# Where the stationary arrays of a two-layer trunk begin in SBUF, taken by 512 bytes

## The chip, the cores and the metric

One Trainium2 chip, of which the kernel uses one core. The metric is the device time of one execution in microseconds (us). All operands are float32 in memory; the large matmuls read them in the rounded form float32r, one pass of the array per matmul.

## The reference

A decoder trunk with 256 tokens and width 2048: one layer of gated linear attention with a SwiGLU, then shared keys and values, one layer of differential attention and a second SwiGLU. Everything is fp32. Nearly all of the arithmetic is the product of the normalised tokens with weight matrices:

```python
def swiglu(h, w_in, w_out):
    g, u = jnp.split(h @ w_in, 2, axis=-1)
    return (jax.nn.silu(g) * u) @ w_out

# layer 0: proj = rms_norm(x) @ w_in   (2048 x 6160), chunked gated attention, @ w_out (2048 x 2048)
# between: kv = rms_norm(x) @ w_kv      (2048 x 4096)
# layer 1: rms_norm(x) @ w_q (2048 x 2048), differential attention, @ w_out (2048 x 2048)
# each layer: x = x + swiglu(rms_norm(x), ffn_w_in, ffn_w_out)   (2048 x 11264, 5632 x 2048)
```

## The kernel before

Weights come from HBM in units of 256 rows by 512 columns (2 tiles of 128 rows, 512 KB) into a ring of four slots, `raw`. To keep fp32 accuracy with float32r, each number is split in two: ScalarE writes the rounded part into `w_hi` (line 945), VectorE the remainder into `w_lo` (line 1311). The activations are split in the same way and stand turned, features on the partitions, in five stationary arrays `[128, 2, tiles, 256]`: the second axis is high part and low part, the last the tokens. They are `xT` (normalised tokens, for all products from the residual stream except the query's), `g_oT` (output of the first attention), `hT` (the hidden layer of both SwiGLUs, 44 tiles), `xT_q` (the tokens for the query) and `d_oT` (output of the second attention). A line of `[128 tokens]` fp32 is 512 bytes in each partition, and a moving tile of `w_hi` or `w_lo` is 2048.

One unit is 2 tiles x 2 halves of the tokens (`tb`) x 3 matmuls: high x high, high x low, low x high. There are 784 units: gla_in 96, gla_out 32, ffn_in0 176, ffn_out0 88, diff_in 96 (of which 32 read `xT_q`), diff_out 32, ffn_in1 176 and ffn_out1 88. `unit` (lines 633 to 642) issues them:

```python
hi = src[:, 0, kt + j, tb * P:(tb + 1) * P]
lo = src[:, 1, kt + j, tb * P:(tb + 1) * P]
nc.tensor.matmul(acc[p][tb][:, :], hi, w_hi[:, slot, j, :], start=(kt + j == 0), stop=False)
nc.tensor.matmul(acc[p][tb][:, :], hi, w_lo[:, slot, j, :], start=False, stop=False)
last = nc.tensor.matmul(acc[p][tb][:, :], lo, w_hi[:, slot, j, :], start=False, ...)
```

The first operand is the stationary one; it is loaded ahead of each matmul by an instruction of its own (LDWEIGHTS, which the profile lists under PEld), and the second moves. In the trace's names `acc<-w_hi,xT` is the moving operand first, then the stationary.

Small matmuls of the attention parts stand between units: `gate_low` (line 727; moving `xT` 256 columns, stationary `a_w` 96 columns of a tile of 384 bytes), `gate_full` (740; moving `a_T`, stationary `w_gate`, 128 columns), `gla_scores` (762, 767, 770), `gla_output` (780 to 782; plain fp32, 512 columns), `scores` (882, 884), `diff_output` (898 to 900). The order on each engine is written out by hand, with semaphores.

Memory is given out in the order of the declarations, each at a multiple of 32 bytes. `place(name, rest)` declares a gap so that the next array begins at the remainder `rest` modulo 512; `ExitStack`s let arrays of later stages take the place of earlier ones. In the program before, `xT` begins at byte 33280, `raw` at 66048, `w_hi` at 82432, `w_lo` at 98816, `hT` at 128512, `g_oT` at 180224, `xT_q` and `d_oT` at 184832 and `a_w` at 161792: all at remainder 0 by 512.

Of the kernel before, what the change touches and what calls it, by code (L numbers as in the profile page):

```python
# [182 lines left out]
def trunk(nc, x_in, attn_norm, gla_w_in, w_alpha2, b_alpha, gla_head_norm, gla_w_out, kv_norm, w_kv, k_norm,  # L183
          diff_norm, diff_w_q, q_norm, lq1, lk1, lq2, lk2, diff_head_norm, diff_w_out, ffn_norm, ffn_w_in,
          ffn_w_out, const_in, out):
    with ExitStack() as ctx:
        def sb(name, shape, dt=F32, stack=ctx):
            return stack.enter_context(nc.sbuf_tensor(name, shape, dt))
# [4 lines left out]
        def place(name, rest, stack=ctx):  # L193

            base = -(-nc.sbuf_base // 32) * 32
            gap = (rest - base) % 512
            if gap:
                sb(name, [P, gap // 4], F32, stack)


        place("gap_x", 0)
        x = sb("x", [P, TB, D])
        xT = sb("xT", [P, 2, KT, S], F32R)
        raw = sb("raw", [P, SLOTS, UNIT_KT, CB])
        w_hi = sb("w_hi", [P, SLOTS, UNIT_KT, CB], F32R)
        w_lo = sb("w_lo", [P, SLOTS, UNIT_KT, CB], F32R)
# [27 lines left out]
        with ExitStack() as s1:  # L234
            tables = sb("tables", [P, C_COLS - C_MASK], F32, s1)
            g_at = sb("g_at", [P, H_G, 3, P], F32, s1)
            g_r = sb("g_r", [P, TB, DV], F32, s1)
            g_v = sb("g_v", [P, 2, TB, HV], F32, s1)
            a_raw = sb("a_raw", [P, KT, RANK], F32, s1)
            a_w = sb("a_w", [P, KT, GATE_ROWS], F32R, s1)  # L240
            a_T = sb("a_T", [GATE_ROWS, S], F32R, s1)
            a_full = sb("a_full", [GATE_ROWS, S], F32, s1)
            gate_raw = sb("gate_raw", [GATE_ROWS, DK], F32, s1)
            w_gate = sb("w_gate", [GATE_ROWS, DK], F32R, s1)
            lam_rows = sb("lam_rows", [P, 4, HD], F32, s1)
            with ExitStack() as s2:
                g_q = sb("g_q", [P, FT, S], F32, s2)
                g_k = sb("g_k", [P, FT, S], F32, s2)
                log_a = sb("log_a", [P, 2, FT // 2 * S], F32, s2)
                cum = sb("cum", [P, 2, S], F32, s2)  # L250
                ends = sb("ends", [P, 2, 8], F32, s2)
                rstd_diag = sb("rstd_diag", [P, TB, P], F32, s2)
                rstd_row = sb("rstd_row", [GATE_ROWS, S], F32, s2)
                ones = sb("ones", [P, GATE_ROWS], F32, s2)
                k_next = sb("k_next", [P, FT, TB, CHUNK], F32, s2)
                k_far = sb("k_far", [P, FT, P], F32, s2)
                q_far = sb("q_far", [P, FT, P], F32, s2)
            place("gap_g", 0, s1)
            g_oT = sb("g_oT", [P, 2, KT, S], F32R, s1)
        with ExitStack() as s1:  # L260
            place("gap_h", 0, s1)
            hT = sb("hT", [P, 2, FKT, S], F32R, s1)
            x_turned = sb("x_turned", [P, 2, TB, CB], F32, s1)
        with ExitStack() as s1:
            d_q = sb("d_q", [P, 2 * H_D, S], F32, s1)
            d_k = sb("d_k", [P, 2 * H_D, S], F32, s1)
            d_at = sb("d_at", [P, H_D, 3, P], F32, s1)
            d_v = sb("d_v", [P, 2, TB, CB], F32, s1)
            probs = sb("probs", [P, 2, 3 * P], F32, s1)
            place("gap_d", 0, s1)  # L270
            with ExitStack() as s2:
                xT_q = sb("xT_q", [P, 2, KT, S], F32R, s2)
            d_oT = sb("d_oT", [P, 2, KT, S], F32R, s1)
            q_squares = sb("q_squares", [P, TB * CB], F32, s1)
            p_squares = sb("p_squares", [P, 6 * P], F32, s1)
            p_turned = sb("p_turned", [P, 6 * P], F32, s1)
# [1474 lines left out]
```

## Time and profile before

| | |
|---|---|
| time, median of 2 runs | 2196.14 us (2196.1 to 2196.19) |
| span of the profiled execution | 2193.8 us |
| TensorE matmul, busy | 2188.1 us (100%), 9720 instructions |
| TensorE weight load, busy | 1808.9 us (82%), 9720 |
| VectorE / ScalarE / GpSimd, busy | 1242.7 (57%) / 1058.2 (48%) / 283.0 us (13%) |
| read from HBM | 414.37 MB, 190 GB/s over the span |
| granted TensorE clock | full in all 40 slices |

Matmuls overlap: the next one starts before the last one's drawn end, so that a busy share of 100% says only that there are no gaps. What the engine delivers is read from the distance between starts.

### The profile page before, as it was taken

The numbers are of one execution on the slowest core, as the hardware profiler recorded it, in microseconds if no ns is written. First come the engines' busy times: TensorE is split into PE (matmuls) and PEld (weight loads), VectorE is DVE, ScalarE is ACT, GpSimd is POOL, SyncE is SP. The second block draws the span as 40 slices with busy tenths as digits, with TensorE's granted clock in tenths as the row PEclk, the third lists the DMA queues.
The fourth block names the chain that finished last, engine by engine and source line by source line (L and its number), as shares of the span: only waits on it lengthen the run. The fifth ranks groups of instructions, "written<-read, shape, count | busy, mean of one in ns | idle before, by whom it ended". The sixth has DMA issues, their size and how long they took to land.

```text
span 2193.8 us, 27239 instructions
## 1 busy us (share of the span) xinstructions
PE 2188.1 (100%) x9720; PEld 1808.9 (82%) x9720; DVE 1242.7 (57%) x1460; ACT 1058.2 (48%) x1428; POOL 283.0 (13%) x563
## 2 busy tenths in 40 slices
PE   9999999999999999999999999999999999999999
PEld 7888788888888888888888888888888888888887
DVE  5665566655555555555566676665555555555443
ACT  6666455444444444444456665554444444444333
POOL 3210334100000000001125333341000000000000
PEclk9999999999999999999999999999999999999999
DMA  8765667666666666666667666676666666666664
GB/s 264 210 189 176 189 202 218 203 215 203 203 202 213 201 202 206 200 205 203 201 202 217 196 207 202 204 223 210 199 207 200 215 200 203 205 210 194 195 193 163
DMA packets 252675, 447.01 MB, mean 204 GB/s; under 512 B 27665, under 2 KB 41969, under 8 KB 252593
## 3 DMA queue, kind: packets, MB, share of 16 engines
q1 hardware_dynamic: 236176, 428.79, 62.2%
q0 software_dynamic: 16240, 17.07, 2.7%
q8 instruction: 49, 0.80, 0.1%
q14 instruction: 34, 0.27, 0.0%
q10 hardware_dynamic: 176, 0.07, 0.0%
HBM read 414.37 MB, written 2.10 MB: 190 GB/s over the span
## 4 chain that ended last, share of the span: by engine, by line
PE 100%; DVE 0%; ACT 0%; issue 0%; POOL 0%; DVEq 0%; ACTq 0%; POOLq 0%
PE acc L641 32%; PE acc L639 32%; PE acc L640 32%; PE acc L651 1%; PE acc L656 0%; PE side L884 0%; PE tps L678 0%; PE side L727 0%; PE side L703 0%; PE side L762 0%; PE side L882 0%; PE side L898 0%; PE side L899 0%; PE side L900 0%; PE side L782 0%; PE side L780 0%
## 5 line engine op out<-in xcount | busy, mean ns | idle before, releaser
L1311 DVE TENSOR_TENSOR w_lo<-raw,w_hi 128x1024 fp32r<-128x1024 f32 x784 | 954.8, 1222 | 835.6 <-ACT w_hi L945 831.3
L945 ACT ACTIVATE w_hi<-raw 128x1024 fp32r<-128x1024 f32 x784 | 827.8, 1059 | 1002.9 <-PE acc L641 994.0
L639 PE MATMUL acc<-w_hi,xT 128*128 128x512 f32 x2016 | 787.6, 391 | 0.0
L641 PE MATMUL acc<-w_hi,xT 128*128 128x512 f32 x2016 | 784.4, 389 | 0.0
L640 PE MATMUL acc<-w_lo,xT 128*128 128x512 f32 x2016 | 784.4, 389 | 0.0
L639 PEld LDWEIGHTS acc<-w_hi,xT 128*128 128x128 f32 x2016 | 378.4, 188 | 79.0 <-issue 0.7
L640 PEld LDWEIGHTS acc<-w_lo,xT 128*128 128x128 f32 x2016 | 378.4, 188 | 78.9 <-issue 0.7
L641 PEld LDWEIGHTS acc<-w_hi,xT 128*128 128x128 f32 x2016 | 378.4, 188 | 78.9
L639 PE MATMUL acc<-w_hi,hT 128*128 128x512 f32 x700 | 272.3, 389 | 0.0
L640 PE MATMUL acc<-w_lo,hT 128*128 128x512 f32 x700 | 272.3, 389 | 0.0
L641 PE MATMUL acc<-w_hi,hT 128*128 128x512 f32 x700 | 272.3, 389 | 0.0
L640 PEld LDWEIGHTS acc<-w_lo,hT 128*128 128x128 f32 x700 | 131.4, 188 | 27.5
L639 PEld LDWEIGHTS acc<-w_hi,hT 128*128 128x128 f32 x700 | 131.4, 188 | 27.3
L641 PEld LDWEIGHTS acc<-w_hi,hT 128*128 128x128 f32 x700 | 131.4, 188 | 27.1
L588 POOL DMA_DIRECT2D x_turned<-scratch x32 | 15.7, 500 | 580.5 <-DVE scratch L1336 580.5
L588 POOL DMA_DIRECT2D tok<-scratch x112 | 54.9, 499 | 143.2 <-DVE scratch L1336 99.5
L1560 DVE TENSOR_TENSOR hT<-tok,hT 128x512 f32 (+1 forms) x44 | 28.4, 688 | 67.1 <-ACT hT L1140 67.1
L1140 ACT ACTIVATE hT<-tok 128x512 f32 (+1 forms) x44 | 25.4, 624 | 64.1 <-DMA tok<-scratch 64.1
L639 PE MATMUL acc<-w_hi,xT_q 128*128 128x512 f32 x128 | 50.6, 396 | 0.0
L639 PE MATMUL acc<-w_hi,g_oT 128*128 128x512 f32 x128 | 50.2, 392 | 0.0
L639 PE MATMUL acc<-w_hi,d_oT 128*128 128x512 f32 x128 | 50.0, 391 | 0.0
L641 PE MATMUL acc<-w_hi,xT_q 128*128 128x512 f32 x128 | 49.9, 390 | 0.0
(204 smaller groups left out, 1372.2 us busy)
## 6 DMA issues: line engine op xcount, KB each, us to landing
raw<-in_ffn_w_in SPq DMA_DIRECT2D x352, 512.0 KB, 3.8
raw<-in_ffn_w_out SPq DMA_DIRECT2D x176, 512.0 KB, 4.7
raw<-in_gla_w_in SPq DMA_DIRECT2D x96, 512.0 KB, 4.3
raw<-in_w_kv SPq DMA_DIRECT2D x64, 512.0 KB, 4.6
raw<-in_gla_w_out SPq DMA_DIRECT2D x32, 512.0 KB, 4.9
raw<-in_diff_w_q SPq DMA_DIRECT2D x32, 512.0 KB, 4.6
raw<-in_diff_w_out SPq DMA_DIRECT2D x32, 512.0 KB, 4.9
tok<-scratch SPq DMA_DIRECT2D x352, 32.0 KB, 2.9
```

Of the source, the lines that this page charges most:

```text
L588: pool.dma_start(dst[g * SQ:(g + 1) * SQ, s], src[s * SQ:(s + 1) * SQ, g]).then_inc(turn_moved[TURN[name, n] % 2], 16)
L639: nc.tensor.matmul(acc[p][tb][:, :], hi, w_hi[:, slot, j, :], start=(kt + j == 0), stop=False)
L640: nc.tensor.matmul(acc[p][tb][:, :], hi, w_lo[:, slot, j, :], start=False, stop=False)
L641: last = nc.tensor.matmul(acc[p][tb][:, :], lo, w_hi[:, slot, j, :], start=False, stop=(kt + j == n_kt - 1))
L651: nc.tensor.matmul(acc[p][tb][:, :], src[:, part, kt + j, tb * P:(tb + 1) * P], w_hi[:, slot, j, :], start=(kt + j == 0 and part == 0), st ...
L945: nc.scalar.activation(w_hi[:, slot, :, :], raw[:, slot, :, :], ACT.Copy).then_inc(hi_done, 1)
L1140: nc.scalar.activation(hidden(0, n, tb), turned(tb), ACT.Copy).then_inc(h_hi, 1)
L1311: nc.vector.tensor_tensor(w_lo[:, slot, :, :], raw[:, slot, :, :], w_hi[:, slot, :, :].bitcast(F32), ALU.subtract).then_inc(lo_done, 1)
L1560: nc.vector.tensor_tensor(hidden(1, n, tb), turned(tb), hidden(0, n, tb).bitcast(F32), ALU.subtract).then_inc(h_lo, 1)
```

## The change

Three more gaps are declared, and two that were there get another remainder. In the program after, `xT` begins at byte 33344 (64 by 512), `raw` at 66560, `w_hi` at 82944, `w_lo` at 99328 (all 0), `hT` at 129280 (256), `g_oT` at 180864 (128), `xT_q` at 185664 (320) and `d_oT` at 185728 (384). Arrays behind them follow: `x_turned` begins at remainder 256, `q_squares`, `p_squares` and `p_turned` at 384. `a_w`, `w_gate` and the operands of the small matmuls move by 512 bytes and keep their remainders, except for `xT` as the moving operand of line 727. No instruction is added or removed, and on every engine the order is the same.

```diff
         place("gap_x", 0)
         x = sb("x", [P, TB, D])
+        place("gap_xT", 64)
         xT = sb("xT", [P, 2, KT, S], F32R)
+        place("gap_raw", 0)
         raw = sb("raw", [P, SLOTS, UNIT_KT, CB])
         w_hi = sb("w_hi", [P, SLOTS, UNIT_KT, CB], F32R)
         w_lo = sb("w_lo", [P, SLOTS, UNIT_KT, CB], F32R)
...
-            place("gap_g", 0, s1)
+            place("gap_g", 128, s1)
             g_oT = sb("g_oT", [P, 2, KT, S], F32R, s1)
         with ExitStack() as s1:
-            place("gap_h", 0, s1)
+            place("gap_h", 256, s1)
             hT = sb("hT", [P, 2, FKT, S], F32R, s1)
             x_turned = sb("x_turned", [P, 2, TB, CB], F32, s1)
...
-            place("gap_d", 0, s1)
+            place("gap_q", 320, s1)
             with ExitStack() as s2:
                 xT_q = sb("xT_q", [P, 2, KT, S], F32R, s2)
+            place("gap_d", 384, s1)
             d_oT = sb("d_oT", [P, 2, KT, S], F32R, s1)
```

## Rows read from the trace of the kernel before

**Rows 1.** The page: span, busy time and share by engine, slices of clock.

```profile
span 2193.8 us, 27239 instructions
PE 2188.1 (100%) x9720; PEld 1808.9 (82%) x9720; DVE 1242.7 (57%) x1460; ACT 1058.2 (48%) x1428; POOL 283.0 (13%) x563
PEclk9999999999999999999999999999999999999999
```

**Rows 2.** The page: the chain that ended last, by engine, by line.

```profile
PE 100%; DVE 0%; ACT 0%; issue 0%; POOL 0%; DVEq 0%; ACTq 0%; POOLq 0%
PE acc L641 32%; PE acc L639 32%; PE acc L640 32%; PE acc L651 1%; PE acc L656 0%; PE side L884 0%; PE tps L678 0%; PE side L727 0%; PE side L703 0%; PE side L762 0%; PE side L882 0%; PE side L898 0%; PE side L899 0%; PE side L900 0%; PE side L782 0%; PE side L780 0%
```

**Rows 3.** Waits, longest first: total us, times, longest.

```profile
ACT w_hi L945 <- PE acc L641: 994.0, 629, 4.3
DVE w_lo L1311 <- ACT w_hi L945: 831.3, 618, 4.9
POOL x_turned L588 <- DVE scratch L1336: 580.5, 2, 528.6
```

**Rows 4.** The page's costliest groups: busy us, mean ns, idle before.

```profile
L1311 DVE TENSOR_TENSOR w_lo<-raw,w_hi 128x1024 fp32r<-128x1024 f32 x784 | 954.8, 1222 | 835.6 <-ACT w_hi L945 831.3
L945 ACT ACTIVATE w_hi<-raw 128x1024 fp32r<-128x1024 f32 x784 | 827.8, 1059 | 1002.9 <-PE acc L641 994.0
L639 PE MATMUL acc<-w_hi,xT 128*128 128x512 f32 x2016 | 787.6, 391 | 0.0
L639 PEld LDWEIGHTS acc<-w_hi,xT 128*128 128x128 f32 x2016 | 378.4, 188 | 79.0 <-issue 0.7
L639 PE MATMUL acc<-w_hi,hT 128*128 128x512 f32 x700 | 272.3, 389 | 0.0
```

**Rows 5.** A stretch of ffn_in0 alone: busy us (count) by engine.

```profile
core 0: us, PE busy (x) PEld busy (x) DVE busy (x) ACT busy (x) POOL busy (x), PEclk, DMA share, GB/s
392.00:860.00 468.00, 468.00 (x2066) 387.51 (x2066) 252.85 (x249) 207.44 (x223) 8.00 (x15) 1.00 0.65 205
```

**Rows 6.** Timeline inside diff_in: start us, duration us, instruction.

```profile
1130.54 0.39 PE L640 MATMUL acc<-w_lo,xT 128*128 128x512 f32 x1
1130.54 0.19 PEld L641 LDWEIGHTS acc<-w_hi,xT 128*128 128x128 f32 x1
...
1130.77 0.39 PE L641 MATMUL acc<-w_hi,xT 128*128 128x512 f32 x1
1130.77 0.19 PEld L639 LDWEIGHTS acc<-w_hi,xT 128*128 128x128 f32 x1
1130.99 0.39 PE L639 MATMUL acc<-w_hi,xT 128*128 128x512 f32 x1
...
1131.22 0.39 PE L640 MATMUL acc<-w_lo,xT 128*128 128x512 f32 x1
...
1131.45 0.39 PE L641 MATMUL acc<-w_hi,xT 128*128 128x512 f32 x1
```

**Rows 7.** Line 640 by stationary array: durations ns min/median/max, starts us.

```profile
L640 PE MATMUL acc<-w_lo,xT x2016: 387/389/398, 32.8 to 1950.3; 128*128 128x512 f32 x184
L640 PE MATMUL acc<-w_lo,hT x700: 389/389/390, 862.4 to 2186.9; 128*128 128x512 f32 x175
L640 PE MATMUL acc<-w_lo,g_oT x128: 389/389/397, 294.0 to 383.0; 128*128 128x512 f32 x128
```

**Rows 8.** Timeline of TensorE's matmuls behind the second gla_scores.

```profile
156.11 0.50 PE L770 MATMUL side<-q_far,k_far 128*128 128x128 f32 x3
156.37 0.48 PE L639 MATMUL acc<-w_hi,xT 128*128 128x512 f32 x1
156.68 0.40 PE L640 MATMUL acc<-w_lo,xT 128*128 128x512 f32 x1
...
157.39 0.39 PE L640 MATMUL acc<-w_lo,xT 128*128 128x512 f32 x1
157.61 0.39 PE L641 MATMUL acc<-w_hi,xT 128*128 128x512 f32 x1
...
158.77 0.39 PE L640 MATMUL acc<-w_lo,xT 128*128 128x512 f32 x1
159.00 0.39 PE L641 MATMUL acc<-w_hi,xT 128*128 128x512 f32 x1
```

**Rows 9.** Lines 727 and 740: durations; the 31 distances between starts of 727.

```profile
L727 PE MATMUL side<-xT,a_w x32: 274/280/284, 38.0 to 41.7; 128*96 128x256 f32 x32
...
L740 PE MATMUL side<-a_T,w_gate x8: 282/283/283, 53.2 to 59.5; 96*128 96x256 f32 x8
...
38.05:41.69 3.64, 3.64 (x32) 3.64 (x31) 3.35 (x5) 3.24 (x5) 0.00 (x0) 1.00 0.53 150
```

**Rows 10.** Timeline of gla_output, 512 columns of plain fp32.

```profile
223.45 1.02 PE L780 MATMUL side<-g_v,g_at 128*128 128x512 f32 x2
224.31 1.02 PE L781 MATMUL side<-g_v,g_at 128*128 128x512 f32 x2
```

## The prediction

> **What bounds the kernel now.** I read the top of the page first [rows 1]: TensorE is busy for 2188.1 of 2193.8 us, and it holds the full granted clock, 9 tenths or more in every slice, so at its 2.4 GHz level. The chain that ended last [rows 2] is TensorE for all of its length, 96% of it in lines 639 to 641, the three matmuls of `unit`. The table of waits [rows 3] has no wait of TensorE among its longest: ScalarE waits 994.0 us for TensorE to free a slot, VectorE 831.3 us for ScalarE, and POOL waits too. So the time is the number of matmuls times the distance from one start to the next, which I call the pitch, and the change can act on the time only through the pitch.
>
> The counts: 784 units of 2 x 2 x 3 matmuls are 9408 matmuls with 512 moving columns. By their stationary array they are xT 512 units, 6144 matmuls; hT 176 units, 2112; g_oT, d_oT and xT_q 32 units, 384 matmuls each. The costliest groups [rows 4] show the same thing in thirds.
>
> The pitch: in a stretch of 468 us that holds nothing else, 2066 matmuls start [rows 5]; with one taken off for the edge that is 226.6 ns. In [rows 6] it is seen singly: starts at 1130.54, .77, .99, 1131.22, .45, each with the weight load of the next matmul beside it. Of all 9408, 226.6 ns each make 2132 us; the other 62 us are the first loads, 312 small matmuls and what they disturb. 512 columns at 2.4 GHz are 213.3 ns, so each matmul takes 13.3 ns more than its columns, 32 cycles. That excess, 9408 x 13.3 ns = 125 us, is the only thing here that an address could change.
>
> **Is the excess fixed?** A matmul's drawn duration here is its pitch and about 162 ns of pipeline (389 against 226.6), so durations show single pitches. By array [rows 7] hT runs from 389 to 390 ns, but xT from 387 to 398: pitches of 225 to 236 ns at one and the same alignment. [rows 8] shows when: after small matmuls with other operands (L770) the starts go 156.68 to 158.77 over nine matmuls, 232.2 ns on average, single ones 220 to 240 by the two digits; after that they stand at 226 to 227. So the excess depends on how the weight load of the next matmul, which begins within 10 ns of each start [rows 6] and lasts 188 ns [rows 4], lies against the moving stream, and the loop falls into a settled pattern at 32 cycles. No DMA or semaphore does that; nothing waits there.
>
> And does the address matter? Every stationary array and the ring begin at 0 mod 512, and each tile of 128 columns is exactly 512 bytes. The one place with 4-byte rounded operands at other remainders is L727: 96 stationary columns, 384 bytes, so the remainder runs through 0, 384, 256, 128 with kt. There the durations go from 274 to 284 ns and never settle [rows 9], while L740, 128 columns at remainder 0, stands at 282 or 283. That speaks for an effect of the remainder, of a few ns either way.
>
> **The change part by part.** It adds and removes no instruction, wait or DMA: both programs list the same 7211 rows in the same order. (1) Padding of 64 + 448 bytes ahead of the ring and 64 to 320 ahead of the others costs no time. (2) xT's, hT's and the other writers on ScalarE and VectorE, and the DMAs that land in x_turned or leave q_squares, work at shifted addresses. Should they become slower, their cover is the 994.0 and 831.3 us of waiting [rows 3]; a unit takes 12 x 226.6 ns = 2.72 us, of which ScalarE's split (1059 ns) and VectorE's (1222 ns) [rows 4] fill less than half. Nothing. (3) The 9408 stationary loads now begin at 64, 128, 256, 320 or 384, cross a 512-byte boundary in each tile, and read against a moving stream that still begins at 0. No row shows 128 stationary columns at such a remainder against 512 moving ones, so I bound it from both sides. Below: 215 ns, what 512 columns take per pass in L780, plain fp32, where two such matmuls start 0.86 us apart and each makes two passes [rows 10]; that is -11.6 ns each, -109 us. Above: the worst single pitch seen, 236 ns, +9.4 ns each, +88 us. Between the ends stand two readings. By L727 the mean is 3.64 us / 31 = 117.4 ns against L740's 119.7 (283 - 163), and a remainder costs or saves some 2 ns: at most +-19 us in all. By the unsettled stretch [rows 8] it is 232.2 ns.
>
> I take the unsettled stretch. Its matmuls are of the very shape that the change touches, with the same two streams, displaced against each other; L727's have 96 columns and 256 moving ones. What is special in the settled state is that both streams begin at 0 and the excess is a whole 32 cycles; displaced by the change, the pattern has no reason to sit at the cheap end of its own range. Price: 232.2 - 226.6 = 5.6 ns. Some 200 matmuls are in unsettled stretches already (some 24 interruptions by the code: 4 gla_scores, 4 gla_output, 8 scores, 4 diff_output, gates and transposes; 6 to 10 matmuls each), so 9200 x 5.6 ns = 51.5 us: xT 33, hT 12, the three small ones 2 each. Span 2193.8 + 51.5 = 2245.3 us; the median of the runs lies 2.3 us over the profiled span, hence 2248 us.
>
> The Trainium skill speaks against any effect: TensorE: Matmul & The Clock Gate, Part 2 (What happens when you issue a matmul), says that TensorE has two independent read ports, so that the next tile's weight load takes no bandwidth from the running matmul. The trace does not fit it well: the same matmul shows 387 to 398 ns with only the phase changed. By that rule the sum would be zero and the time 2196 us.
>
> **The rivals.**
> Same time (a third): the loop settles again at a whole 32 cycles, because what locks it is the ratio of the two streams and not where they begin, or the remainder is not seen at all. For it: xT, hT and g_oT all settle at the same median of 389 [rows 7], and their bases differ by 512 bytes modulo 1024. Time 2196 us, with L727's +-2 ns 2177 to 2215.
> Faster: the displaced streams meet less often. The excess is a collision, each one a cycle or two; remainders that keep the streams apart would cut it. Place: `unit`; price: from -2 ns (225, the lowest duration of xT) to -11.6 ns each. It decides the sign with xT alone, which has 65% of the matmuls: at xT 225 and the rest unchanged 2184 us; at 215 everywhere 2087. For it: 274 ns in L727. Against it: of the unsettled pitches hardly one is below the settled one.
> Worse than forecast: settling at the far end, 236 ns: +88 us, 2284 us.
> Mixed: five remainders need not agree. xT decides; hT is a third of it.
>
> **How the numbers follow.** Displaced and dearer (2215 to 2290, middle 2248): 0.50. Same by settling or by indifference (2180 to 2215): 0.35. Faster (2087 to 2180): 0.13. Worse than 2290: 0.02. The range of 8 in 10 reaches from 2184, with the same-time case whole, to 2290. 2% is 44 us, about what a measurement can tell: the border lies at 2240, just under my middle, so of the dearer case some three quarters are slower by over 2%: 0.38. Within 2%: the rest of it and the same-time case, 0.48. Faster by over 2%, under 2152: 0.14 with the tail. The forecast is of a loss that stands near the border of being called one.
>
> **What would show it.** The counts of instructions stay, TensorE stays at 100% and the full clock. Right, if the pitch in the stretch of [rows 5] is near 232 and the durations of L639 to L641 with xT spread or sit near 394 instead of 389; each array has its own duration, so each remainder is read by itself, and hT's row says whether 256 does as 64 does. Wrong, if these rows stay at 389 (same) or fall towards 378 (faster). If TensorE begins to wait for DVE or a DMA, step (2) was wrong. If ScalarE's or VectorE's durations change while the pitch stays, the addresses matter to them alone.

## The result, and the profile after

The changed kernel takes 2242.73 us (median of 2 runs, 2242.68 to 2242.78) against 2196.14 us: a ratio of 1.0212, 95% interval 1.0182 to 1.0242. It is slower beyond doubt; whether by more than 2% is left open by the interval. The profiled span went from 2193.8 to 2240.8 us, by 47.0 us.

The page of after, its counterpart to [rows 1] and [rows 2]:

```profile
span 2240.8 us, 27239 instructions
PE 2235.1 (100%) x9720; PEld 1806.6 (81%) x9720; DVE 1242.8 (55%) x1460; ACT 1057.4 (47%) x1428; POOL 281.0 (13%) x563
PEclk9999999999999999999999999999999999999999
PE 100%; DVE 0%; ACT 0%; issue 0%; POOL 0%; DVEq 0%; ACTq 0%; POOLq 0%
```

The same instructions, the same clock, VectorE and ScalarE as busy as before to within a microsecond. The waits of the two splitting engines, beside [rows 3], grew by 45.4 and 39.5 us, about what the kernel grew:

```profile
ACT w_hi L948 <- PE acc L644: 1039.4, 634, 4.3
DVE w_lo L1314 <- ACT w_hi L948: 870.8, 622, 5.3
```

All of it is in the distance between the starts of TensorE's matmuls, the pitch. Line 643 of after is line 640 of before; durations in ns, min/median/max, by stationary array (beside [rows 7]). A duration is the pitch and some 162 ns:

```profile
L643 PE MATMUL acc<-w_lo,xT x2016: 388/394/399, 33.6 to 1997.3; 128*128 128x512 f32 x184
L643 PE MATMUL acc<-w_lo,hT x700: 387/389/390, 886.2 to 2234.0; 128*128 128x512 f32 x175
L643 PE MATMUL acc<-w_lo,g_oT x128: 389/393/405, 301.5 to 392.6; 128*128 128x512 f32 x128
L643 PE MATMUL acc<-w_lo,xT_q x128: 392/394/398, 1216.0 to 1310.1; 128*128 128x512 f32 x128
L643 PE MATMUL acc<-w_lo,d_oT x128: 390/393/405, 1413.4 to 1504.5; 128*128 128x512 f32 x128
```

hT, now at remainder 256, is where it was ([rows 7]: 389). The others are dearer. Two stretches of after by engine, the first with xT (beside [rows 5]), the second with hT:

```profile
core 0: us, PE busy (x) PEld busy (x) DVE busy (x) ACT busy (x) POOL busy (x), PEclk, DMA share, GB/s
400.00:870.00 470.00, 470.00 (x2016) 376.75 (x2015) 247.06 (x245) 201.82 (x219) 8.71 (x18) 1.00 0.68 199
885.00:1120.00 235.00, 235.00 (x1038) 194.56 (x1037) 123.43 (x129) 100.91 (x112) 23.54 (x48) 1.00 0.66 203
```

With one start taken off for the edge, 470 / 2015 = 233.2 ns with xT and 235 / 1037 = 226.6 ns with hT. The distances between successive starts in the two traces give each array's share (29 of them in each trace, longer than 250 ns and next to small matmuls, are left out of the means):

| array | remainder | mean pitch before | after | matmuls | share of the loss |
|---|---|---|---|---|---|
| xT | 64 | 226.8 ns | 233.3 ns | 6144 | 40.0 us |
| hT | 256 | 226.7 | 226.7 | 2112 | 0.1 |
| g_oT | 128 | 226.7 | 232.4 | 384 | 2.2 |
| xT_q | 320 | 227.2 | 233.3 | 384 | 2.3 |
| d_oT | 384 | 226.8 | 232.4 | 384 | 2.1 |

46.7 us of the 47.0. The table already suggests a period: 256 is as 0, 320 as 64, 384 as 128. In cycles of 2.4 GHz, the level of the granted clock, 512 columns take 512, before they took 544, with xT at 64 now 560.

### The profile page after: what moved, and what is told of

It is laid out like the page before. It is cut to its first block, busy times and chain, and to the rows that moved or that the text cites. A ratio compares the mean times of both kernels' runs of the same rounds, so it can differ in the third digit from the quotient of the medians.

```text
span 2240.8 us, 27239 instructions
## 1 busy us (share of the span) xinstructions
PE 2235.1 (100%) x9720; PEld 1806.6 (81%) x9720; DVE 1242.8 (55%) x1460; ACT 1057.4 (47%) x1428; POOL 281.0 (13%) x563
## 4 chain that ended last, share of the span: by engine, by line
PE 100%; DVE 0%; ACT 0%; issue 0%; POOL 0%; DVEq 0%; ACTq 0%; POOLq 0%
PE acc L644 32%; PE acc L643 32%; PE acc L642 32%; PE acc L654 1%; PE acc L659 0%; PE side L887 0%; PE tps L681 0%; PE side L730 0%; PE side L706 0%; PE side L765 0%; PE side L885 0%; PE side L903 0%; PE side L901 0%; PE side L902 0%; PE side L783 0%; PE side L784 0%
## 5 line engine op out<-in xcount | busy, mean ns | idle before, releaser
L1314 DVE TENSOR_TENSOR w_lo<-raw,w_hi 128x1024 fp32r<-128x1024 f32 x784 | 954.7, 1222 | 874.3 <-ACT w_hi L948 870.8
L948 ACT ACTIVATE w_hi<-raw 128x1024 fp32r<-128x1024 f32 x784 | 827.0, 1059 | 1047.1 <-PE acc L644 1039.4
L642 PE MATMUL acc<-w_hi,xT 128*128 128x512 f32 x2016 | 797.8, 396 | 0.0
L644 PE MATMUL acc<-w_hi,xT 128*128 128x512 f32 x2016 | 794.7, 394 | 0.0
L643 PE MATMUL acc<-w_lo,xT 128*128 128x512 f32 x2016 | 794.7, 394 | 0.0
L642 PE MATMUL acc<-w_hi,xT_q 128*128 128x512 f32 x128 | 51.2, 400 | 0.0
L642 PE MATMUL acc<-w_hi,g_oT 128*128 128x512 f32 x128 | 50.9, 398 | 0.0
L644 PE MATMUL acc<-w_hi,g_oT 128*128 128x512 f32 x128 | 50.5, 395 | 0.0
```

The source lines that it names most:

```text
L948: nc.scalar.activation(w_hi[:, slot, :, :], raw[:, slot, :, :], ACT.Copy).then_inc(hi_done, 1)
L1314: nc.vector.tensor_tensor(w_lo[:, slot, :, :], raw[:, slot, :, :], w_hi[:, slot, :, :].bitcast(F32), ALU.subtract).then_inc(lo_done, 1)
```

## The experiments

**Which array, and whose displacement?** Three kernels. The first is the changed one with xT alone put back:

```diff
-        place("gap_xT", 64)
+        place("gap_xT", 0)
```

> The changed kernel with xT alone back at remainder 0; g_oT 128, hT 256, xT_q 320 and d_oT 384 stay. In the trace of after the pitch with xT is 233.3 ns against 226.7 before, hT's is unchanged. Theory D (the stationary array's own displacement sets its own pitch): xT's 6144 matmuls fall back by 6.6 ns each, -40.5 us, to about 2202 us; durations of the xT rows 389 again, g_oT and d_oT still near 395, xT_q near 395. Rival W (the loss comes from elsewhere in the shifted layout: writers, DMAs, x_turned): the xT rows stay at 394 and the time near 2240 us.

Measured: 2203.24 us, ratio 1.0032 (1.002 to 1.0045). Its line 643:

```profile
L643 PE MATMUL acc<-w_lo,xT x2016: 387/389/398, 33.4 to 1958.1; 128*128 128x512 f32 x184
L643 PE MATMUL acc<-w_lo,g_oT x128: 390/393/404, 294.7 to 385.8; 128*128 128x512 f32 x128
L643 PE MATMUL acc<-w_lo,xT_q x128: 392/394/398, 1192.5 to 1286.7; 128*128 128x512 f32 x128
```

39.5 us of the loss went with one number; xT is cheap again while the others stay dear. So each array sets its own pitch, and x_turned and q_squares, still shifted here, have no part. xT's own writers were put back together with xT; the next two runs, where they are shifted and nothing is lost, clear them too.

The second puts all five at 256:

```diff
-        place("gap_xT", 64)
+        place("gap_xT", 256)
...
-            place("gap_g", 128, s1)
+            place("gap_g", 256, s1)
...
-            place("gap_q", 320, s1)
+            place("gap_q", 256, s1)
...
-            place("gap_d", 384, s1)
+            place("gap_d", 256, s1)
```

> All five stationary arrays at remainder 256, the ring at 0. Each tile of 512 bytes then crosses a 512-byte boundary. Theory D with a period of 256 bytes: every array at 226.7 ns, time 2196 us, all durations 389. Rival B (a tile that crosses a 512-byte boundary is dearer, and hT's 389 in after has another cause): xT's pitch stays above 230 ns and the time above 2230 us.

Measured: 2196.18 us, ratio 1.0001 (0.9991 to 1.001), with xT as in the kernel before:

```profile
L643 PE MATMUL acc<-w_lo,xT x2016: 387/389/398, 32.9 to 1950.6; 128*128 128x512 f32 x184
```

A tile of 512 bytes that crosses a 512-byte boundary costs nothing here, and rival B falls. The time fits a period of 256 bytes.

The third puts the stationary arrays at 64 and the ring there too:

```diff
-        place("gap_raw", 0)
+        place("gap_raw", 64)
...
-            place("gap_g", 128, s1)
+            place("gap_g", 64, s1)
...
-            place("gap_h", 256, s1)
+            place("gap_h", 64, s1)
...
-            place("gap_q", 320, s1)
+            place("gap_q", 64, s1)
...
-            place("gap_d", 384, s1)
+            place("gap_d", 64, s1)
```

> All five stationary arrays at 64 and raw, w_hi and w_lo at 64 too, so that nothing is displaced between the two operands. Theory D (the displacement between stationary and moving operand): 226.7 ns everywhere, 2196 us. Rival S (the stationary tile's own place against a boundary of 256 bytes): 233.3 ns everywhere, 9400 x 6.6 ns = +62 us, about 2258 us.

Measured: 2196.14 us, ratio 1.0 (0.999 to 1.001), and at line 643:

```profile
L643 PE MATMUL acc<-w_lo,xT x2016: 386/389/398, 33.4 to 1950.9; 128*128 128x512 f32 x184
```

xT is at 64 as in the changed kernel and is cheap. What costs is not the stationary array's address by itself but its displacement against the moving operand. Rival S falls. (At displacements of 4 and 16 bytes the displacement alone does not give the pitch, as the second map shows.)

**A map.** The kernel before with blocks of further matmuls at its end (they write to PSUM that nobody reads; each block has 64). The same code serves the later maps, with lists in place of single displacements:

```diff
+            def probe(n, stat, move, cols=P, rows=CB, out_=None):
+
+                whole = hT[:, :, :, :].rearrange("q a k s -> q (a k s)")
+                ring = w_hi[:, :, :, :].rearrange("q s j n -> q (s j n)")
+                for i in range(n):
+                    at = (i % 8) * P + stat // 4
+                    on = (i % 4) * CB + move // 4
+                    nc.tensor.matmul(out_[0:cols, 0:rows], whole[:, at:at + cols], ring[:, on:on + rows], start=True, stop=True)
+
+            for n, args in enumerate(PROBES):
+                probe(PROBE_N, *args, out_=(tps, side)[n % 2][0])
```

> The kernel before with 27 blocks of 64 further matmuls at its end, stationary from hT and moving from w_hi, results thrown away: remainders of the stationary tile 0 to 480 in steps of 32 against a moving tile at 0, then pairs with the moving tile at 64, 128 or 256, then fewer stationary or moving columns. Theory D: the pitch repeats with 256 (0 and 256 at 226.7 ns, 64 and 320 at 233.3, 128 and 384 near 232), 64 against 64 is as 0 against 0, and 0 against 64 is as 192 against 0. Rival S: the pitch goes by the stationary remainder alone whatever the moving one is. If the excess over 213.3 ns comes from reads of the weight load that meet the moving stream, it falls with the number of stationary columns (96, 64, 32: 10, 6.7, 3.3 ns), and stays 13.3 ns with 256 moving columns; if it is a fixed cost of changing the weights it stays 13.3 ns in all of them. The profiled time is the 2194 us of before and 27 x 64 x about 0.22 us, so some 380 us more.

The blocks of the timeline, start and drawn length in us; the distance between the starts of two blocks over 64 is the mean pitch, the first few matmuls included. First the stationary tile at 0, 32, 64, 96, 128, then further on at 192, 224, 256, 288:

```profile
2190.67 14.68 PE L941 MATMUL tps<-w_hi,hT 128*128 128x512 f32 x64
2205.19 15.09 PE L941 MATMUL side<-w_hi,hT 128*128 128x512 f32 x64
2220.11 15.10 PE L941 MATMUL tps<-w_hi,hT 128*128 128x512 f32 x64
2235.04 15.15 PE L941 MATMUL side<-w_hi,hT 128*128 128x512 f32 x64
2250.03 15.04 PE L941 MATMUL tps<-w_hi,hT 128*128 128x512 f32 x64
...
2279.84 14.83 PE L941 MATMUL tps<-w_hi,hT 128*128 128x512 f32 x64
2294.51 15.09 PE L941 MATMUL side<-w_hi,hT 128*128 128x512 f32 x64
2309.43 14.68 PE L941 MATMUL tps<-w_hi,hT 128*128 128x512 f32 x64
2323.95 15.09 PE L941 MATMUL side<-w_hi,hT 128*128 128x512 f32 x64
```

The pitches given for the maps are means over the single distances of a block from the fifth on, when most loops have settled, so that they differ from these by some tenths:

| stationary at | 0, 256 | 32, 288 | 64, 320 | 96, 352 | 128, 384 | 160, 416 | 192, 448 | 224, 480 |
|---|---|---|---|---|---|---|---|---|
| pitch, ns | 226.7 | 233.4 | 233.4 | 234.3 | 232.5 | 233.4 | 228.9 | 233.3 |

Both halves agree within 0.1 ns: the period is 256 bytes, and 64 and 128 give the pitches that xT and g_oT have in the kernel. With the moving tile elsewhere (stationary first): 64 against 64 settles at 226.7 after ten unsettled distances, 0 against 64 gives 228.9, as 192 against 0, 128 against 64 gives 233.3, as 64 against 0, 0 against 128 gives 232.3 and 0 against 256 gives 226.7. Apart from the last output in the first 5 us, nothing else runs on the core, as this stretch of the map by engine shows (columns as in [rows 5]):

```profile
2210.00:2575.00 365.00, 365.00 (x1641) 286.21 (x1640) 0.00 (x0) 0.00 (x0) 0.00 (x0) 1.00 0.00 1
```

VectorE, ScalarE, GpSimd and the DMAs are idle, and the pitches are those of the full kernel: no other engine takes part in the effect.

Neither reading of the cause held. The excess should have shrunk with the stationary columns if it came from the load's reads, or stayed at 13.3 ns in all blocks if it were a fixed cost of changing the weights. These are the blocks with 96, 64 and 32 stationary columns at displacement 0:

```profile
2501.71 14.89 PE L941 MATMUL side<-w_hi,hT 128*96 128x512 f32 x64
2516.44 14.87 PE L941 MATMUL tps<-w_hi,hT 128*64 128x512 f32 x64
2531.15 14.99 PE L941 MATMUL side<-w_hi,hT 128*32 128x512 f32 x64
2545.97 7.83 PE L941 MATMUL tps<-w_hi,hT 128*128 128x256 f32 x64
```

230.0, 229.9 and 231.7 ns: more than with 128 columns, although a load of 32 is a quarter of one of 128. A count of reads of the load that meet the stream does not give that, nor does a fixed cost. (With 64 stationary columns at 64 it is 231.2.)

**Which load meets which stream?** A second map, with alternating displacements.

> The kernel before with 30 blocks of 64 further matmuls at its end, results thrown away. First block: stationary and moving tile both at 0, then both at 64, in turn: a matmul's own operands are never displaced, but the load of the next weights is, by 64, against the stream that runs meanwhile. Second block: the own operands are displaced by 64 each time, the next load and the running stream never. Theory N (the next weights' load meets the running stream): first block 229 to 233 ns (displacements +64 and -64 in turn), second 226.7. Rival O (a matmul's own two operands): first 226.7, second 229 to 233. The same with 128 in blocks 3 and 4: by N 232 and 226.7, by O the reverse. Blocks 5 and 6 write to two PSUM banks in turn: 226.7 and 233.4 if PSUM has no part in it. Then displacements of 4 to 24 and 240 to 252 bytes: if the grain is 16 bytes, 4 to 12 are as 0; if it is the element they differ. Then fewer moving columns, 448, 384, 320 and 128, at 0 and 64: an excess that belongs to the load stays at 13.3 and 20 ns as long as the load fits beneath it, one that belongs to the moving columns shrinks with them; at 128 columns the load is the longer one. Last 96 and 32 stationary columns at several displacements: the earlier map had 230.0 ns for 96 and 231.7 for 32 at 0; no displacement is expected to give 96 columns less than 226.7.

The first five blocks, then those with the stationary tile at 252, the moving tile at 16 and the moving tile at 4:

```profile
2190.74 14.98 PE L942 MATMUL tps<-w_hi,hT 128*128 128x512 f32 x64
2205.56 14.97 PE L942 MATMUL side<-w_hi,hT 128*128 128x512 f32 x64
2220.38 14.78 PE L942 MATMUL tps<-w_hi,hT 128*128 128x512 f32 x64
2234.99 14.88 PE L942 MATMUL side<-w_hi,hT 128*128 128x512 f32 x64
2249.71 14.71 PE L942 MATMUL tps<-w_hi,hT 128*128 128x512 f32 x64
...
2367.82 14.67 PE L942 MATMUL tps<-w_hi,hT 128*128 128x512 f32 x64
2382.33 14.99 PE L942 MATMUL side<-w_hi,hT 128*128 128x512 f32 x64
2397.15 15.31 PE L942 MATMUL tps<-w_hi,hT 128*128 128x512 f32 x64
```

Own operands never displaced but neighbours by 64 one way and the other: 231.7. Own displaced by 64, neighbours not: 231.6. With 128: 228.4 and 230.0. Each theory had said 226.7 for one block of each pair; none of the four is there. So neither pairing alone is what is paid for. Either one of the two displaced is enough, or it is something that all four blocks share: in each of them successive tiles of one operand also alternate by 64 or 128 against each other. No run separates these. Two PSUM banks in turn change nothing (226.7 after eight unsettled distances, and 233.4). The grain is the element: 4 bytes give 232.4, 8 give 230.7, 12 give 230.1, 16 give 233.4, 24 give 230.0, 240 give 228.3, 252 give 226.7. A moving tile at 4 gives 236.7, the dearest so far, and one at 16 gives 231.6.

These last two bound the reading of e3. The moving tile 4 bytes ahead is the same displacement by 256 as the stationary tile at 252, yet it takes 236.7 ns against 226.7; for 16 and 240 it is 231.6 against 228.3. Displacement alone gives the pitch at steps of 64 bytes; below that the place of the moving tile counts as well.

With fewer moving columns, the excess over the columns at 2.4 GHz:

| moving columns | 512 | 448 | 384 | 320 | 256 |
|---|---|---|---|---|---|
| excess at 0, ns | 13.3 | 16.0 | 13.5 | 13.3 | 13.2 |
| excess at 64, ns | 20.0 | 15.5 | 16.7 | 13.3 | 11.1 |

(512 and 256 from the first map.) The excess at 0 doesn't shrink with the moving columns, but what 64 bytes cost does depend on them, and at 256 and 448 columns 64 is the cheaper one. At 128 moving columns both give 111.7 ns, 58.3 over the columns. With 96 stationary columns 0, 32, 64, 128 and 192 give 230.0, 228.9, 228.3, 231.7 and 233.4: of these five 64 is best. "Same remainder is best" thus holds for 128 by 512 and not as a rule.

**Is there a cheaper displacement?**

> The kernel before with 64 blocks of 48 further matmuls at its end, results thrown away: the stationary tile at each displacement from 0 to 252 bytes in steps of 4 (one element) against a moving tile at 0. The earlier maps had 226.7 ns at 0 and 252, 228.3 at 240, 229.0 at 192, 232.4 at 4, 230 at 24, 233.4 at 32 and 64, 234.3 at 96. Theory L (the loop settles at a whole 32 cycles of 2.4 GHz near 0, and no constant displacement is cheaper): the lowest pitch of all 64 is 226.7 ns, at 0 and its neighbours below (252, perhaps 248). Rival C (the excess is a count of meetings that a well chosen displacement avoids): at least one displacement under 225 ns, which the main loop could use; the span would then be 9408 times the difference shorter.

Blocks of 48, here 0, 4 and 8 bytes, then 120 and 124, then 252:

```profile
2190.71 11.05 PE L942 MATMUL tps<-w_hi,hT 128*128 128x512 f32 x48
2201.60 11.32 PE L942 MATMUL side<-w_hi,hT 128*128 128x512 f32 x48
2212.76 11.24 PE L942 MATMUL tps<-w_hi,hT 128*128 128x512 f32 x48
...
2525.48 11.05 PE L942 MATMUL tps<-w_hi,hT 128*128 128x512 f32 x48
2536.37 11.28 PE L942 MATMUL side<-w_hi,hT 128*128 128x512 f32 x48
...
2892.86 11.05 PE L942 MATMUL side<-w_hi,hT 128*128 128x512 f32 x48
```

Of 64 displacements seven settle at 226.7 ns, or 544 cycles: 0, 120, 132 (after six unsettled distances), 144, 156, 228 and 252. None is below. The others lie between 228.3 and 236.9, and the largest group, some 30 of them, within 0.3 ns of 560 cycles, 233.3 ns. Theory L's lowest pitch holds and rival C falls for constant displacements; that 120, 132, 144, 156 and 228 are as cheap as 0 was not expected, since only 0 and its neighbours below had been named.

**Do the maps hold in the kernel?** All five arrays at 192 (the changed kernel with 192 in each of the five `place` calls), and, in another kernel, w_lo alone moved:

```diff
-        place("gap_xT", 64)
+        place("gap_xT", 192)
...
-            place("gap_h", 256, s1)
+            place("gap_h", 192, s1)
```

> All five stationary arrays at remainder 192, the ring at 0. If the map of plain repeated matmuls (229.0 ns at 192) carries over to the loop of three matmuls: +2.3 ns for 9200 matmuls, +21 us, 2217 us, xT's durations near 391. If the loop's own pattern matters (w_hi, w_lo, w_hi moving in turn): another time between 2196 and 2258 us, since every displacement but 0 and 256 lay between 229 and 234 ns.

Measured: 2216.36 us, ratio 1.0092 (1.0075 to 1.0109), where the map had said 2217; xT's stretch in it starts 2046 matmuls in 468 us, 228.9 ns:

```profile
392.00:860.00 468.00, 468.00 (x2046) 384.04 (x2045) 251.18 (x250) 205.29 (x223) 8.71 (x18) 1.00 0.69 202
```

The durations misled here: the pitches run 226, 229, 232 in turn, and each of the three lines of the loop always catches the same one (medians with xT of 394, 388 and 392 ns at lines 642, 643 and 644). The count of starts did not mislead. The block at 192 in the first map settles into the same three distances.

```diff
+        place("gap_lo", 64)
         w_lo = sb("w_lo", [P, SLOTS, UNIT_KT, CB], F32R)
+        place("gap_tok", 0)
```

> The kernel before with w_lo alone moved by 64 bytes; the five stationary arrays, raw and w_hi stay at 0. One moving tile in three is then displaced by 64 against its own stationary tile and against the load of the next. If each matmul pays for itself, a third of 9408 matmuls pays what 0 against 64 showed in the map, 228.9 - 226.7 = 2.2 ns: +7 us, 2203 us. If one displaced matmul in three throws the whole loop out of its settled pattern, as the mixed pairs of the second map did (231.7 ns): +5 ns each, about 2242 us.

Measured: 2244.32 us, ratio 1.022 (1.0203 to 1.0238). One moving tile in three is displaced and every array pays, hT too: 2027 starts in 470 us, 232.0 ns:

```profile
400.00:870.00 470.00, 470.00 (x2027) 380.30 (x2026) 248.78 (x246) 202.96 (x220) 6.30 (x14) 1.00 0.68 200
L642 PE MATMUL acc<-w_lo,hT x700: 388/395/398, 880.9 to 2235.4; 128*128 128x512 f32 x175
```

The loss is that of the whole loop and not of a third: a matmul doesn't pay for itself alone, the pattern of the sequence does. This is as large as the whole change, from one array whose stationary partners were never moved. The second reading of the two had said about 2242.

**A mixed layout.** The last try for something faster than both kernels.

> The kernel before with 64 blocks of 48 further matmuls at its end, results thrown away. Each block repeats the pattern of the main loop, high x high, high x low, low x high: the stationary high part at 0, the stationary low part at b, the moving high part at 0, the moving low part at d, with b and d from 0 to 224 in steps of 32. Known points: b = d = 0 is the kernel before (226.7 ns); b = 0, d = 64 is the run with w_lo moved (its loop ran at 232.0 ns), so this block should give 232 as well. Theory L (with tiles at multiples of 512 bytes no layout of the four streams settles under a whole 32 cycles): the lowest of the 64 is 226.7 ns. Rival C (a mixed layout can string together the cheap single pitches of 224 ns that the settling stretches show): some block under 226 ns, and a kernel with that b and d would gain 9400 times the difference, 6 us for each 0.67 ns.

```profile
2190.24 11.04 PE L942 MATMUL tps<-w_hi,hT 128*128 128x512 f32 x48
2201.12 11.36 PE L942 MATMUL side<-w_hi,hT 128*128 128x512 f32 x48
2212.32 11.30 PE L942 MATMUL tps<-w_hi,hT 128*128 128x512 f32 x48
2223.46 11.26 PE L942 MATMUL side<-w_hi,hT 128*128 128x512 f32 x48
```

These are b = 0 with d = 0, 32, 64 and 96: 226.7, 233.6, 232.0, 231.1. The third is the loop with w_lo at 64, and it gives that kernel's 232.0; its single distances (235, 233, 230, 237, 241, 224, 226, 229 ns and on, in a cycle of 15) are those of e8's stretch from 400 to 860 us, one by one and within 1 ns. The lowest of the 64 is b = d = 0. One other comes down to it, b = 128 with d = 160:

```profile
2601.58 11.09 PE L942 MATMUL side<-w_hi,hT 128*128 128x512 f32 x48
```

Its first seven distances lie at 231 to 236 ns, and from the eighth on it stands at the same 226.7. Nothing settles under 226.7, so no kernel was built from it. No layout that was tried beats the one before; several tie with it.

## Why the prediction was right, and where only by luck

**What bounds the kernel, and that only the pitch can move: right.** TensorE stayed at 100% with the full clock, no wait took its place, and 46.7 of 47.0 us are in the pitches of the 9408 matmuls.

**Step (1), padding costs nothing, and step (2), the shifted writers: right.** In e2 and e3 the layout is padded and shifted and the time is 2196.2 and 2196.1 us. The two splits take 1059 and 1222 ns in after as in before.

**Step (3), the price: right in sum, wrong in its parts.** I took 5.6 ns for every array, from the unsettled stretch, 51.5 us: xT 33, hT 12, the small ones 2 each. Measured: xT 40.0, hT 0.1, the small ones 2.1 to 2.3. xT's price was 6.7 ns and not 5.6, so its term was too small by 7 us, and hT's price was nothing instead of 5.6, its term too large by 12. The two errors partly cancel, to 51.5 us forecast and 46.7 measured; that luck makes 2248 against 2242.7 us flatter the working. The failed step is the one that treats every remainder but 0 alike: the period is 256 bytes, and hT at 256 isn't displaced at all. [rows 9] could have hinted at it only weakly, since 96 columns behave otherwise.

**The mechanism: half right.** That the excess depends on how two streams of TensorE lie against each other, and that the change displaces them, is shown by e3 (the same 64 costs nothing when both are moved) and by the maps with idle engines. That the displaced loop stays unsettled, at the mean of the unsettled stretch, is not what happened: it settles too, into another pattern. With xT at 64 the mean is 560 cycles, again a whole multiple of 16, in the kernel nearly all single pitches are 233 or 234, and in the map's block they repeat as 231, 236. The mean of the unsettled stretch (232.2) lay near the mean over the 64 displacements of e6 (232.1), which made it a usable price; no run shows that this is more than a coincidence.

**What the excess is** stays open. I had put it down to the next load's reads against the running stream. e4 and e5 speak against the simple form: 32 stationary columns cost more than 128 (231.7 against 226.7 ns), and the block with only the own pair displaced is as dear as the one with only the neighbouring pair displaced. The runs tie it to the sequence of displacements at the grain of one element, with a period of 256 bytes and settled values that are, in 45 of the 64 blocks of e6, within 0.3 ns of a multiple of 8 cycles of 2.4 GHz. What in the chip has this period wasn't found.

**The two read ports.** The Trainium skill (TensorE: Matmul & The Clock Gate, Part 2, What happens when you issue a matmul) says that TensorE reads the weights and the moving operand through two independent ports, so that the load takes no bandwidth from the running matmul. The prediction drew from it that addresses cannot matter, hence 2196 us. The page does not say that, and the conclusion does not hold here: the change cost 2.1% by addresses alone, and the maps show the same pitches with every other engine idle. Whether the two reads meet at the ports or behind them, or not at all, no run shows.

**The rivals.** "Same time" was true of hT. Its argument, that arrays whose bases differ by 512 bytes settle alike, was true but said nothing of 64: 512 is two periods. "Faster" found nothing in 64 constant and 63 mixed layouts. "Mixed: five remainders need not agree, xT decides" was the true picture and had no chance of its own in my list; it should have been the main case with the dear price on xT.

## What to carry to other kernels

Where one instruction fills the span, its pitch in a quiet stretch, counted by starts, is worth comparing with its ideal, and a map of one parameter can be hung behind a finished kernel: 27 blocks of 64 matmuls added 0.38 ms to one execution, and their 229.0 ns at 192 forecast the whole kernel e7 to within 1 us; the mixed pairs of e5 forecast e8 to within 2.4 us. For float32r matmuls of 128 by 512 with tiles of whole 512 bytes, keep all stationary and all moving arrays at the same remainder by 256 bytes (run with all at 0, all at 64, and 256 against 0); here misplacing xT alone or w_lo alone cost some 2%. For other shapes measure, since for 96 stationary or 256 moving columns another displacement was cheaper.

## What the runs showed of the hardware that I had not expected

- The period of 256 bytes at a grain of 4: 226.7 ns at displacement 0, 232.4 at 4, 226.7 at 252, 120, 132, 144, 156 and 228, up to 236.9 at 164 (e6).
- It is not symmetric in its two operands: 4 bytes on the stationary side give 232.4, on the moving side 236.7, although the latter is the same displacement as 252 on the stationary side, 226.7. So it is not a matter of displacement alone below steps of 64 bytes.
- The order of single pitches repeats too: the loop with w_lo at 64 runs through the same cycle of 15 distances, 224 to 241 ns, in the full kernel and in a block with the other engines idle.
- A third of the moving tiles displaced by 64 costs the whole loop 5.3 ns per matmul, nearly as much as displacing all stationary tiles (6.6 with xT at 64).
- Fewer stationary columns don't make a matmul of 512 moving columns cheaper: 128, 96, 64, 32 take 226.7, 230.0, 229.9, 231.7 ns at displacement 0.
